# A two-layer decoder trunk on one core: identity transposes at the start, half transfers of the last weights, and another order of the last additions and the final norm

## What is computed

```python
# layer 0
x = x + sliding_window_attention(rms_norm(x, attn_norm[0]), ...)    # 16 heads, window 128
x = x + (silu(h @ w_gate) * (h @ w_up)) @ w_down                    # h = rms_norm(x), width 2816
# layer 1
x = x + pooling_mixer(rms_norm(x, pool_norm[0]), pool_w, pool_scale)
t = rms_norm(x, moe_norm[0])
combine = top-2-of-8 softmax gates of t @ w_router                  # (256, 8)
out = zeros_like(t)
for e in range(8):                                                  # width 3584
    out = out + combine[:, e:e+1] * ((silu(t @ w_gate[e]) * (t @ w_up[e])) @ w_down[e])
x = x + out
return rms_norm(x, final_norm)
```

## Time and profile before

| | |
|---|---|
| median of three runs | 1188.87 us (1187.67, 1188.87, 1188.97) |
| profiled execution, its own time | 1187.06 us |
| its span on the core | 1185.2 us |
| PE busy | 1155.3 us (97%) |
| DVE, ACT, POOL busy | 190.6, 129.3, 15.3 us |
| HBM read | 400.61 MB, mean 340 GB/s |
| mean granted TensorE clock | 0.994 of full speed |

### The profile page before, as it was taken

One profiled execution on the slowest core, in us unless ns is written; L12 is line 12 of the kernel. 1 busy time (PEld: TensorE's weight loads), 2 busy tenths in 40 slices (PEclk: granted clock), 3 DMA queues, 4 the chain that ended last, 5 costly groups with the idle time before them and its releaser, 6 DMA issues.

```text
span 1185.2 us, 15075 instructions
## 1 busy us (share of the span) xinstructions
PE 1155.3 (97%) x6514; PEld 557.3 (47%) x6515; DVE 190.6 (16%) x382; ACT 129.3 (11%) x280; POOL 15.3 (1%) x52
## 2 busy tenths in 40 slices
PE   8999999999999999999999999999999999999995
PEld 7647888874474342344333335333333533333331
DVE  2642000000042120110121011011101102110102
ACT  1352000010031110000111000011100001010002
POOL 1300000000000000000000000000000000000000
PEclk9999999999999999999999999999999999999998
DMA  8434046536655799999999999999999999999992
GB/s 303 196 123 197 2 176 251 233 140 245 247 232 235 322 402 364 417 431 429 429 431 430 392 429 429 431 431 427 426 433 431 427 430 429 433 427 427 432 430 98
DMA packets 18838, 402.93 MB, mean 340 GB/s; under 512 B 3264, under 2 KB 3264, under 8 KB 4032
## 3 DMA queue, kind: packets, MB, share of 16 engines
q1 hardware_dynamic: 18752, 401.67, 80.7%
HBM read 400.61 MB, written 1.05 MB: 339 GB/s over the span
## 4 chain that ended last, share of the span: by engine, by line
PE 89%; DMA 7%; DVE 2%; ACT 1%; issue 0%; SPq 0%; DVEq 0%; ACTq 0%
PE bank L1321 31%; PE bank L1413 13%; PE bank L1122 13%; PE bank L1302 8%; PE bank L1156 6%; PE bank L1434 4%; DMA ring<-moe_w_up 3%; DMA ring<-moe_w_down 3%; PE bank L1080 2%; PE bank L1024 2%; PE bank L1281 1%; PE bank L1263 1%; PE bank L1000 1%; PE bank L1251 1%; PE bank L1286 1%; PE bank L1379 1%
## 5 line engine op out<-in xcount | busy, mean ns | idle before, releaser
L1321 PE MATMUL bank<-ring,arena 128*64 128x448 f32 x2048 | 391.3, 540 | 1.5 <-DMA ring<-moe_w_up 1.2
L1321 PEld LDWEIGHTS bank<-ring,arena 128*64 128x64 f32 x2048 | 145.1, 137 | 246.6 <-issue 244.6
L1413 PE MATMUL bank<-ring,arena 128*64 128x512 f32 x896 | 199.0, 599 | 6.6 <-DMA ring<-moe_w_down 4.8
L1122 PE MATMUL bank<-ring 128*128 128x256 f32 (+1 forms) x768 | 152.8, 362 | 0.0
L1122 PEld LDWEIGHTS bank<-ring 128*128 128x128 f32 x768 | 136.0, 190 | 17.0 <-issue 0.5
L1413 PEld LDWEIGHTS bank<-ring,arena 128*64 128x64 f32 x896 | 64.2, 138 | 129.8 <-issue 120.4
L1302 PE MATMUL bank<-ring,arena 128*32 128x448 f32 x1024 | 99.7, 541 | 0.0
L1156 PE MATMUL bank<-ring,arena 128*128 128x512 f32 x176 | 75.7, 592 | 0.0
L877 DVE TENSOR_TENSOR arena<-bank,arena 128x448 f32<-128x448 f32 x32 | 20.0, 625 | 334.6 <-PE bank L1321 334.6
L1302 PEld LDWEIGHTS bank<-ring,arena 128*32 128x32 f32 x1024 | 31.5, 110 | 66.6 <-issue 66.6
L1156 PEld LDWEIGHTS bank<-ring,arena 128*128 128x128 f32 x176 | 33.4, 190 | 41.7 <-issue 41.6
(11 more groups left out here) (161 smaller groups left out, 530.3 us busy)
## 6 DMA issues: line engine op xcount, KB each, us to landing
ring<-moe_w_gate SPq DMA_DIRECT2D x32, 3584.0 KB, 22.4
ring<-moe_w_up SPq DMA_DIRECT2D x32, 3584.0 KB, 27.2
ring<-moe_w_down SPq DMA_DIRECT2D x32, 3584.0 KB, 28.0
ring<-ffn_w_gate SPq DMA_DIRECT2D x2, 3072.0 KB, 10.1
ring<-ffn_w_up SPq DMA_DIRECT2D x2, 3072.0 KB, 10.2
ring<-ffn_w_down SPq DMA_DIRECT2D x2, 3072.0 KB, 14.5
ring<-ffn_w_gate SPq DMA_DIRECT2D x2, 2560.0 KB, 13.7
ring<-ffn_w_up SPq DMA_DIRECT2D x2, 2560.0 KB, 19.3
```

Of the source, the lines that this page charges most:

```text
L1122: last = mm(bank[u % 4][:, half * S + ts.start:half * S + ts.stop], w[:, k, f:f + P], hT[:, k, ts], start=k == 0, stop=k == KD - 1)
L1321: last = mm(bank[2 * (j % 2) + up][64 * h:64 * h + 64, 0:FJ], xg[:, k, side:side + BASE], w[:, k, h, :], start=k == 0, stop=k == KD - 1)
L1413: last = mm(bank[2][64 * h:64 * h + 64, :], hg[:, i0 + i, half * BASE:half * BASE + BASE], w[:, i, h * BANK:h * BANK + BANK], start=d == 0 ...
```

## The change

There are four edits.

1. Between the transposes of tile 0 and tile 1 PE does six transposes of the identity.
2. For the last expert (it = 7) chunks 9, 10 and 11 are moved in two transfers each, of 4 and of 3 of the seven 1024-column blocks. The second transfer raises a semaphore of its own, `late_half`, and PE waits for it ahead of the fifth block.
3. PE's `final` no longer branches on `ext`: it always uses all 128 partitions, one matmul for each tile and column half. So that the unused halves of `y` hold finite numbers, POOL fills all of `y` with zeros before the experts. The branches on `over` (a second round of experts, not taken here) are turned round, so that the path without it comes first.
4. At the very end DVE adds all four halves one behind the other. ACT takes tile 0's norm as soon as its two halves are there, then tile 1's, and scales both tiles afterwards. The product of tile 0 with `final_b` moves from DVE to POOL, and DVE and ACT wait for it (`out_scaled`) before they scale. Each tile has its own `out_ready`.

```diff
+        def in_halves(it, c):
+            return isinstance(it, int) and it == NE - 1 and c > 8
...
-                sp.dma_start(ring[s][:, :], w.rearrange("o p n -> (o p) n")).then_inc(full[s], 16)
+                w = w.rearrange("o p n -> (o p) n")
+                if in_halves(it, c):
+                    at = 4 * D
+                    sp.dma_start(ring[s][:, 0:at], w[:, 0:at]).then_inc(full[s], 16)
+                    sp.dma_start(ring[s][:, at:SLOT], w[:, at:SLOT]).then_inc(late_half[c - 8], 16)
+                else:
+                    sp.dma_start(ring[s][:, :], w).then_inc(full[s], 16)
...
-            nc.gpsimd.memset(comb[:, :, NIT:NIT + 1], 0.0).then_inc(zeros_ready, 1)
+            pool.wait_ge(pooled, 2 * T)
+            own.step(nc.gpsimd.memset(y[:, :, :], 0.0))
+            own.link(nc.gpsimd.memset(comb[:, :, NIT:NIT + 1], 0.0))
+            pool.sem_inc(zeros_ready, 1)
...
+            pool.wait_ge(final_in, 16)
+            pool.wait_ge(final_x, 2)
+            nc.gpsimd.tensor_tensor(out_rows(0), xres[:, 0, :], final_b, ALU.mult).then_inc(out_scaled, 1)
...
             for t in range(T):
                 norm(4, t)
+            for t in range(T):
                 act.wait_ge(rstd_ready, t + 1)
+                if t == 0:
+                    act.wait_ge(out_scaled, 1)
                 nc.scalar.activation(out_rows(t)[:, BANK:D], out_rows(t)[:, BANK:D], ACT.Copy,
-                                     scale=rstd[:, t:t + 1]).then_inc(out_ready, 1)
+                                     scale=rstd[:, t:t + 1]).then_inc(out_ready[t], 1)
...
+            def final(n):
+                dve.wait_ge(xadd_done, 4 * n + 4)
+                for t in range(T):
+                    for h in range(2):
+                        dve.wait_ge(scat_done, 2 * (n * T + t) + h + 1)
+                        hs = slice(h * BANK, h * BANK + BANK)
+                        nc.vector.tensor_tensor(xres[:, t, hs], bank[(6, 0)[t] + h][:, :], xres[:, t, hs],
+                                                ALU.add).then_inc(final_x, 1)
...
             dve.wait_ge(final_in, 16)
+            dve.wait_ge(final_x, 2 * T)
+            own.link(nc.vector.tensor_tensor(out_rows(1), xres[:, 1, :], final_b, ALU.mult))
             for t in range(T):
                 dve.wait_ge(std_ready, 4 * T + t + 1)
                 nc.vector.reciprocal(rstd[:, t:t + 1], std[:, t:t + 1]).then_inc(rstd_ready, 1)
                 dve.wait_ge(rstd_ready, t + 1)
+                if t == 0:
+                    dve.wait_ge(out_scaled, 1)
...
-            transposes(0, 0)
+            transposes(0, 0, (0,))
+            for _ in range(6):
+                nc.tensor.transpose(bank[7][:, 0:P], ident[:, :], ident[:, :])
+            transposes(0, 0, (1,))
...
                     for i in range(ID):
+                        if i == 4 and in_halves(it, c):
+                            pe.wait_ge(late_half[d], 16)
...
             def final(n):
-                ext = pe.value_load(flags[0:1, n:n + 1], min_val=0, max_val=1)
+
                 pe.wait_ge(sc_ready, n + 1)
+                pe.wait_ge(xg_ready, 2 * n + 2 if n > NE else 2 * n)
                 pe.wait_ge(y_ready, 2 * n + 2)
                 pe.wait_ge(yx_ready, 2 * n + 2)
-                pe.wait_ge(xg_ready, 2 * n + 2 if n > NE else 2 * n)
-                scatter(ext, n, 0, 6)
-                scatter(ext, n, 1, 0)
+                for t in range(T):
+                    for h in range(2):
+                        mm(bank[(6, 0)[t] + h][:, :], sc[:, T * h + t, :], y[:, h, :],
+                           start=True, stop=True).then_inc(scat_done, 1)
```

More of the change, by code:

```diff
@@ L199, in trunk_kernel @@
         full = [sem(f"full{i}") for i in range(SLOTS)]
+        late_half = [sem(f"late_half{d}") for d in range(4)]
         pool_step = sem("pool_step")
@@ L277, in trunk_kernel @@
         xadd_done = sem("xadd_done")
-        out_ready = sem("out_ready")
+        final_x = sem("final_x")
+        out_scaled = sem("out_scaled")
+        out_ready = [sem(f"out_ready{t}") for t in range(T)]
         out_sent = sem("out_sent")
@@ L402, in _ @@
             for t in range(T):
-                sp.wait_ge(out_ready, 2 * t + 2)
+                sp.wait_ge(out_ready[t], 2)
                 sp.dma_start(out[0].rearrange("(t p) d -> t p d", p=P)[t], out_rows(t)).then_inc(out_sent, 16)
@@ L474, in norm @@
                     act.wait_ge(x_in[t], 16)
+                elif q == 4:
+                    act.wait_ge(final_x, 2 * t + 2)
                 else:
@@ L603, in _ @@
             over = act.value_load(flags[0:1, OVER:OVER + 1], min_val=0, max_val=1)
-            with act.If(over > 0):
+            with act.If(over < 1):
+                pass
+            with act.Else():
                 with act.Fori(NE, NIT, 1) as it:
                     expert(it)
-            with act.Else():
-                pass
             preload(ACT.Sqrt)
@@ L934, in expert @@
                     dve.sem_inc(yx_ready, 2)
-            def final(n, t):
-                if t == 0:
-                    dve.wait_ge(xadd_done, 4 * n + 4)
-                scattered(n, t, (6, 0)[t])
-                dve.wait_ge(xadd_done, 4 * n + 2 * t + 6)
-                dve.sem_inc(x_ready, 1)
+            def final(n):
[6 more added lines that the diff above has]
+                                                ALU.add).then_inc(final_x, 1)
             for it in range(NE):
@@ L945, in _ @@
             over = dve.value_load(flags[0:1, OVER:OVER + 1], min_val=0, max_val=1)
-            with dve.If(over > 0):
+            with dve.If(over < 1):
+                final(NE)
+            with dve.Else():
                 dispatch(column(NE), 0)
@@ L950, in _ @@
                     expert(it, looped=True)
-                final(NIT, 0)
-            with dve.Else():
-                final(NE, 0)
-            dve.wait_ge(x_ready, 3 * T + 1)
+                final(NIT)
             dve.wait_ge(final_in, 16)
-            own.step(nc.vector.tensor_tensor(out_rows(0), xres[:, 0, :], final_b, ALU.mult))
-            with dve.If(over > 0):
-                final(NIT, 1)
-            with dve.Else():
-                final(NE, 1)
-            dve.wait_ge(x_ready, 3 * T + 2)
+            dve.wait_ge(final_x, 2 * T)
+            own.link(nc.vector.tensor_tensor(out_rows(1), xres[:, 1, :], final_b, ALU.mult))
             for t in range(T):
-                if t == 1:
-                    own.step(nc.vector.tensor_tensor(out_rows(1), xres[:, 1, :], final_b, ALU.mult))
                 dve.wait_ge(std_ready, 4 * T + t + 1)
-                own.wait()
                 nc.vector.reciprocal(rstd[:, t:t + 1], std[:, t:t + 1]).then_inc(rstd_ready, 1)
                 dve.wait_ge(rstd_ready, t + 1)
+                if t == 0:
+                    dve.wait_ge(out_scaled, 1)
                 nc.vector.tensor_scalar(out_rows(t)[:, 0:BANK], out_rows(t)[:, 0:BANK], rstd[:, t:t + 1],
-                                        None, ALU.mult).then_inc(out_ready, 1)
+                                        None, ALU.mult).then_inc(out_ready[t], 1)
         @block.tensor
@@ L1459, in _ @@
             over = pe.value_load(flags[0:1, OVER:OVER + 1], min_val=0, max_val=1)
-            with pe.If(over > 0):
+            with pe.If(over < 1):
+                final(NE)
+            with pe.Else():
                 gather(NE, 0)
@@ L1464, in _ @@
                 final(NIT)
-            with pe.Else():
-                final(NE)
 _INS = ["x", "norm_gains", "attn_w_qkv", "attn_sinks", "attn_w_o", "ffn_w_gate", "ffn_w_up",
```

## The result

| | before | changed |
|---|---|---|
| median of six runs | 1188.27 us | 1179.74 us |
| lowest and highest | 1186.63 to 1189.83 | 1178.70 to 1182.88 |
| profiled execution, its span | 1185.2 us | 1181.1 us |

A forecast was written before the change was run, and what follows sets the result against it. PE bounds the kernel through the mixer, the weight stream through the experts, then a chain after the last landing. Overlap 3.56, scatter 0.80, end 0.85 and clock 1.9 make 7.1 us off 1188.87: 1181.8, range 1179.0 to 1185.6.

The forecast's parts named there:

- three signs of being wrong: PE's first group of chunk 11 starts at the last landing, landings move later, or the clock falls somewhere new.
- two thirds of the clock's 2.85 us: Start and chunk 11: full clock brings 1.15 and 1.70 us; the median was credited with 1.9.
- the last sign of being wrong: Anywhere in the kernel: the prediction is wrong if PE's clock falls at a new place; no size given.
- The overlap of 3.56 us: Chunk 11: PE does 16 of 28 records before the second half lands, saving 3.56 us.
- the clock of 1.70: Chunk 11: PE's clock stays up, so its records take 6.23 us and not 7.93, saving 1.70.
- The rival that both land together: Chunk 11: both halves arrive at once, the overlap is lost, 2.4 us are left, 1186.4 us; chance 0.09.
- that of a cost for each transfer: Last chunks: three more transfers each add their latency, chunk 11 lands 9.6 us later, 1193.2 us; chance 0.03.
- The gain of 0.80: From DVE's copy of `y` to PE's scatter: without the branch 0.10 us in place of 0.90.
- the sign of under 0.2 us: Expected in the changed profile: under 0.2 us from DVE's copy of `y` to PE's scatter.
- The rival of the clock falling before the scatter: Scatter: PE's clock falls while idle, the last addition comes 3.4 us later, 1185.2 us; chance 0.06.
- The 7.5 us: The end: 7.5 us from PE's first scatter matmul to the last scaling, 1.16 less than before.
- the first rival: The end: POOL's product holds up DVE's, so scaling ends at 8.05 us, not 7.5; total 1182.4; chance 0.20.

The follow-up runs named there:

- e7: The changed kernel without the six identity transposes at the start; 1181.74 us, ratio to before 0.9953.
- the second: The changed kernel unaltered, measured again against the kernel before as reference for two kernels with a part taken out; 1180.96 us, ratio 0.9945.

## Why the prediction was right

The terms of the sum were mostly found in the profile. But of the prediction's three signs of being wrong two came true in it: the landings moved later, by 2.44 us, and the clock fell at a new place, the router. That the median was met all the same is in part luck, as the last paragraph of this section says.

**The six transposes.** 1.15 us was forecast where the clock had fallen, and 1.16 was measured; the queries' chunk did not hold PE, and the shift was carried to the router unchanged. What was mis-sized is how often. I counted two thirds of the clock's 2.85 us, from three stretches of one profile. At the start the fall is rarer (one profile of five without the transposes), so this part is worth less than the 0.8 us it was given; taking it out cost 0.8 us in the median, which is not told from nothing. A fall at the router had no rival and no price; only the last sign of being wrong covers it. It was the largest single loss in the changed kernel's profile.

**The halves.** The forecast had the first landing 4.84 us after chunk 10 and PE done 2.67 after the last. The trace has 1161.96 after 1157.11, so 4.85, and 2.84. The overlap of 3.56 us and the clock of 1.70 were both there, 5.13 of the 5.26 us. PE's one wait was 2.06 us long and not 1.2, and the clock stayed all the same; in e7 it fell after 1.95. Taking the halves out cost 3.75 us. The rival that both land together fell with the two landings, and so did that of a cost for each transfer.

**The scatter.** 0.10 us were forecast for the handover and 0.25 measured, against 0.90 in the profile before. The gain of 0.80 was 0.65 for that pair of profiles, and the sign of under 0.2 us was missed. In the four profiles with the old scatter the handover is between 0.90 and 2.14 us and in three of them the clock is low, so the scatter and the end together are worth some 2.65 us on the mean of the profiles, where I gave them 1.65 and the median of the two alone gave 1.4. The rival of the clock falling before the scatter described these three, and never a kernel with the new scatter.

**The end.** POOL's product was put at 2.34 us and took 2.36; ACT's two norms ended 5.9 us after PE's first matmul as worked out (6.0). The 7.5 us became 7.86, since DVE's product was held, as the first rival has it. That rival said 8.05; the scalings began at 6.5 us where it had 6.6, and ACT's two took 1.34 us and not 1.44. The outputs cost nothing: from the last scaling to the end of the span 3.8 us in both, so the 0.3 for the second output was not there.

**The sum.** 3.56 + 0.80 + 0.85 + 1.9 = 7.1 us; the first comparison gave 8.5 and the second 6.6. The 1.9 for the clock was worked out from two places of one profile. By the mean clocks it is about 3 us, and two places that the forecast priced at nothing had a share in it: the router took up to 2.9 us away, and the old scatter, late and mostly at the low clock, gave more back than its term. That the total still came close is in this part luck. What stays open is why the three parts alone gave only 2.5 us. The old scatter and its clock may account for 1.2 us, the difference between the profile before and the mean of the four, and the router's clock differs from run to run; the intervals of the single parts are 2.1 to 3.3 us wide, so no more of it can be told.

## What to carry to other kernels

When a stream of weights is the bound, what is worth cutting stands ahead of the stream, where each microsecond moves all of it, and behind its last landing. The latter is cut by making the last transfers small: two pieces brought PE from 7.97 us behind the last landing to 2.84 and five to 1.1, at under 0.1 us for each further transfer. Let an engine's last work start without a branch of its own between the wait and the work. And where PE's clock falls, ask of each stretch how often it falls over several profiles, since a fill at one place says nothing of the next.

## What was not expected

- The clock fell with PE busy all the time: 2.00 of 2.00 us from 350 to 352 in the changed kernel, with the fall at 352.3, in products of eight columns and a few identity transposes. In the profile before PE was as busy there and the clock stayed. In the changed kernel's it was at 0.50 through 6.5 us in which PE was busy for 6.47, with the gather's 96-column matmuls.
- With a branch between PE's wait and its first matmul, the matmul came 0.90 to 2.14 us after the release, with a packet of 0.02 MB of the instruction queue in each of the four profiles. Six instructions of dead code did not change the median.
- DVE's product of two SBUF operands, started while POOL multiplied from SBUF, ended 1.08 us after POOL's did, whether it had started 0.69 or 1.20 us before that.
